# Two-block transformer kernel: rotated query and key rows turned by DMA through HBM and VectorE's 32x32 block transpose

## The reference

```python
h = rmsnorm(x, g_mix)
z = h @ w_in                                    # 1024 -> 5888
aq, ak, av, rq, rk, rv, rg, ga, gb = jnp.split(z, SPLIT_POINTS, axis=-1)

aq = rope_half(aq.reshape(B, S, 8, 64), pos)    # 8 query heads of 64
ak = rope_half(ak.reshape(B, S, 2, 64), pos)    # 2 key heads of 64
ya = sliding_window_sink_attention(aq, ak, av, sinks) @ w_a

rq = retention_rotation(rq.reshape(B, S, 4, 128), pos)
rk = retention_rotation(rk.reshape(B, S, 4, 128), pos) * (128 ** -0.5)
r = chunkwise_retention(rq, rk, rv)             # scores rq.rk per chunk of 128 rows
```

## Time and profile before

| what | us |
|---|---|
| median of 3 runs | 1018.91 (1018.56 to 1019.53) |
| profiled execution, first to last instruction (span) | 1017.5 |
| PE busy | 1010.2 (99% of the span) |
| DVE busy | 715.8 (70%) |
| ACT busy | 506.0 (50%) |
| POOL busy | 170.8 (17%) |
| SP queue's DMA packets, share of 16 engines | 52.8% |

### The profile page before, as it was taken

One profiled execution on the slowest core, in us unless ns is written; L12 is line 12 of the kernel. 1 busy time (PEld: TensorE's weight loads), 2 busy tenths in 40 slices (PEclk: granted clock), 3 DMA queues, 4 the chain that ended last, 5 costly groups with the idle time before them and its releaser, 6 DMA issues.

```text
span 1017.5 us, 13670 instructions
## 1 busy us (share of the span) xinstructions
PE 1010.2 (99%) x5709; PEld 856.6 (84%) x5709; DVE 715.8 (70%) x819; ACT 506.0 (50%) x624; POOL 170.8 (17%) x129
## 2 busy tenths in 40 slices
PE   9999999999999999999999999999999999999997
PEld 8888788888888888888788888888887899899786
DVE  5767755766566565786755767888877767789974
ACT  6545544355444445454564355444467545554352
POOL 0520010000000000430000011000000139259730
PEclk9999999999999999999999999999999999999999
DMA  9763444555556555554444457556553654345451
GB/s 339 246 218 130 166 166 143 178 175 198 183 198 195 178 169 183 186 207 166 158 134 164 166 145 259 203 196 205 190 188 135 223 192 166 124 164 146 116 187 42
DMA packets 98046, 181.29 MB, mean 178 GB/s; under 512 B 8680, under 2 KB 13888, under 8 KB 97856
## 3 DMA queue, kind: packets, MB, share of 16 engines
q1 hardware_dynamic: 97808, 180.32, 52.8%
q10 hardware_dynamic: 176, 0.09, 0.0%
HBM read 177.02 MB, written 1.05 MB: 175 GB/s over the span
## 4 chain that ended last, share of the span: by engine, by line
PE 96%; DMA 2%; DVE 0%; ACT 0%; SPq 0%; issue 0%; DVEq 0%; ACTq 0%
PE bank L745 14%; PE bank L747 12%; PE bank L748 12%; PE bank L1072 11%; PE bank L770 9%; PE bank L774 8%; PE bank L781 8%; PE bank L1076 6%; PE bank L1154 2%; DMA raw<-in_w_in 2%; PE bank L1378 1%; PE bank L943 1%; PE bank L752 1%; PE bank L762 1%; PE bank L1365 1%; PE bank L772 1%
## 5 line engine op out<-in xcount | busy, mean ns | idle before, releaser
L1863 DVE TENSOR_TENSOR w_lo<-arena,w_hi 128x2048 fp32r<-128x2048 f32 (+1 forms) x80 | 185.3, 2325 | 107.5 <-ACT w_hi L1466 107.1
L1863 DVE TENSOR_TENSOR w_lo<-raw,w_hi 128x2048 fp32r<-128x2048 f32 (+1 forms) x78 | 181.2, 2333 | 92.1 <-ACT w_hi L1466 92.0
L1466 ACT ACTIVATE w_hi<-raw 128x2048 fp32r<-128x2048 f32 (+1 forms) x83 | 157.0, 1892 | 105.4 <-PE bank L748 71.5
L1466 ACT ACTIVATE w_hi<-arena 128x2048 fp32r<-128x2048 f32 (+1 forms) x80 | 151.3, 1891 | 105.1 <-PE bank L748 81.3
L1072 PE MATMUL bank<-hT,w_hi 128*128 128x512 f32 x504 | 123.4, 391 | 0.0
L745 PE MATMUL bank<-w_hi,hT 128*128 128x512 f32 (+1 forms) x296 | 114.1, 386 | 0.0
L1072 PEld LDWEIGHTS bank<-hT,w_hi 128*128 128x128 f32 x504 | 92.2, 188 | 17.5
L2465 POOL TENSOR_TENSOR rstd<-mean,const 128x1 f32<-128x1 f32 (+1 forms) x16 | 9.1, 578 | 557.5 <-DVE mean L1872 388.4
L748 PE MATMUL bank<-w_hi,hT 128*128 128x512 f32 (+1 forms) x256 | 97.9, 382 | 0.0
L747 PE MATMUL bank<-w_lo,hT 128*128 128x512 f32 (+1 forms) x256 | 97.9, 382 | 0.0
L770 PE MATMUL bank<-w_hi,hT 128*128 128x512 f32 (+1 forms) x216 | 84.0, 391 | 0.5 <-ACT arena L1478 0.5
(11 more groups left out here) (350 smaller groups left out, 1899.0 us busy)
## 6 DMA issues: line engine op xcount, KB each, us to landing
arena<-in_w_in SPq DMA_DIRECT2D x22, 1024.0 KB, 5.0
raw<-in_w_in SPq DMA_DIRECT2D x20, 1024.0 KB, 5.0
arena<-in_w_up SPq DMA_DIRECT2D x16, 1024.0 KB, 5.3
raw<-in_w_up SPq DMA_DIRECT2D x16, 1024.0 KB, 5.2
arena<-in_w_down SPq DMA_DIRECT2D x16, 1024.0 KB, 5.0
raw<-in_w_down SPq DMA_DIRECT2D x16, 1024.0 KB, 5.0
raw<-in_e_w_in SPq DMA_DIRECT2D x6, 1024.0 KB, 5.1
arena<-in_e_w_in SPq DMA_DIRECT2D x6, 1024.0 KB, 5.1
```

Source lines behind the costliest of these rows:

```text
L1466: act.activation(w_hi[:, p % SPLIT_RING, :, 0:n], raw_at(p)[:, :, 0:n], copy).then_inc(hi_ready, 1)
L1863: dve.tensor_tensor(w_lo[:, s, :, 0:n], raw_at(p)[:, :, 0:n], w_hi[:, s, :, 0:n].bitcast(F32), ALU.subtract).then_inc(lo_ready, 1)
```

## The change

The rotated rows are no longer turned by PE. The rotations write their results in blocks of 32 columns (block number outermost). The SP queue stores them to two internal tensors in HBM (`r_bounce`, 1 MB for both tiles in one DMA; `a_bounce`, 384 KB for each tile). It then fetches them again with every block of 32 columns in its own strip of 32 partitions (`fetch_blocks`: four DMAs of 32 partitions each for the retention rows, and four for each tile of the attention rows). DVE then turns every 32x32 block in place with one instruction for all retention rows (128 x 2048 elements to `rT`) and one for all attention rows (128 x 1536 to `aT`). `rqT`, `rkT`, `aqT` and `akT` are the same places as before. The 16 and 12 transposes of PE and the seven copies of ACT and DVE from PSUM are gone. PE's window 5 waits for `rT_ready` ahead of the retention scores and for `aT_ready` ahead of the attention scores.

The bounce DMAs are put between weight loads of the SP queue (`blocks_moved`), and the two DVE transposes between weight splits. Everything is done once in each of the two layers, and a layer moves 1.75 MB out and 1.75 MB back.

```diff
--- before.py
+++ after.py
@@ -30,6 +30,9 @@
 RET_HEADS = 4
 RET_QK = 128
 RET_V = 256
+BLOCK = 32
+BLOCKS = P // BLOCK
+A_SLOTS = PAIRS + KV_HEADS
 
 ATT2_HEADS = 4
 ROT2 = 32
@@ -278,7 +281,13 @@
         rkT = area(14336, RET_HEADS, SEQ)
         s_far = area(15360, RET_HEADS * P)
         s_ret = area(15872, T, RET_HEADS * P)
-        ak_twice = area(16896, T, KV_HEADS * 2 * HEAD)
+        rT = area(13312, 2 * RET_HEADS, SEQ)
+        aT = area(11776, PAIRS + KV_HEADS, SEQ)
+        r_moved = area(5632, T * BLOCKS, 2 * RET_HEADS * BLOCK)
+        a_moved = area(15360, T * BLOCKS, A_SLOTS * BLOCK)
+        a_rows = area(16896, T, BLOCKS * A_SLOTS * BLOCK)
+        r_bounce = nc.dram_tensor("r_bounce", [T * P, 2 * RET_HEADS * RET_QK], F32, kind="Internal").ap()
+        a_bounce = nc.dram_tensor("a_bounce", [T * P, BLOCKS * A_SLOTS * BLOCK], F32, kind="Internal").ap()
         probs = area(18432, 2, 384)
         probsT = area(19200, 2, 384)
         rg_tanh = z_ga[:, :, 0:512]
@@ -390,13 +399,12 @@
         turned_lo = sem("turned_lo")
         rot_done = [sem(f"rot_done{t}") for t in range(T)]
         rope_done = [sem(f"rope_done{t}") for t in range(T)]
...
@@ -572,8 +580,10 @@
             o.mark(eng.tensor_tensor(bp[:, :, :, 1], zp[:, :, :, 0], sin, ALU.mult))
             between(1)
             o.settle()
-            o.mark(eng.tensor_tensor(zp[:, :, :, 0], ap[:, :, :, 0], bp[:, :, :, 0], ALU.subtract))
-            eng.tensor_tensor(zp[:, :, :, 1], ap[:, :, :, 1], bp[:, :, :, 1], ALU.add).then_inc(rot_done[t], 1)
+            to = z.rearrange("p (b n d e) -> p n b d e", b=BLOCKS, n=heads, e=2)
+            a5, b5 = (v.rearrange("p n (b d) e -> p n b d e", b=BLOCKS) for v in (ap, bp))
+            o.mark(eng.tensor_tensor(to[:, :, :, :, 0], a5[:, :, :, :, 0], b5[:, :, :, :, 0], ALU.subtract))
+            eng.tensor_tensor(to[:, :, :, :, 1], a5[:, :, :, :, 1], b5[:, :, :, :, 1], ALU.add).then_inc(rot_done[t], 1)
             eng.wait_ge(rot_done[t], l + 1)
 
         def rotate_halves(eng, o, l, t, tmp):
@@ -593,11 +603,12 @@
             o.mark(eng.tensor_tensor(b4[:, :, 0, :], z[:, :, 1, :], sin, ALU.mult))
             o.mark(eng.tensor_tensor(b4[:, :, 1, :], z[:, :, 0, :], sin, ALU.mult))
             o.settle()
-            twice = ak_twice[:, t, :].rearrange("p (v c e d) -> p v c e d", v=KV_HEADS, c=2, e=2)
+            to = a_rows[:, t, :].rearrange("p (c e s d) -> p s c e d", c=2, e=2, s=A_SLOTS)
+            aq, bq = (v[:, 0:Q_HEADS, :, :].rearrange("p (i c) e d -> p i c e d", c=2) for v in (a4, b4))
             for e, op in ((0, ALU.subtract), (1, ALU.add)):
-                o.mark(eng.tensor_tensor(z[:, 0:Q_HEADS, e, :], a4[:, 0:Q_HEADS, e, :], b4[:, 0:Q_HEADS, e, :], op))
+                o.mark(eng.tensor_tensor(to[:, 0:PAIRS, :, e, :], aq[:, :, :, e, :], bq[:, :, :, e, :], op))
                 for c in range(2):
-                    last = eng.tensor_tensor(twice[:, :, c, e, :], a4[:, Q_HEADS:, e, :], b4[:, Q_HEADS:, e, :], op)
+                    last = eng.tensor_tensor(to[:, PAIRS:, c, e, :], a4[:, Q_HEADS:, e, :], b4[:, Q_HEADS:, e, :], op)
                     if e == 0 or c == 0:
                         o.mark(last)
             last.then_inc(rope_done[t], 1)
@@ -655,10 +666,40 @@
                     sp.dma_start(raw_at(p)[:, :, 0:piece.shape[2]], piece).then_inc(raw_landed[RAW_SLOTS[p]], 16)
                 n[0] += 1
 
+            def store_rows(dst, src, done):
+
+                sp.dma_start(dst, src).then_inc(done, 16)
+
+            def fetch_blocks(dst, src, done):
+
+                for b in range(BLOCKS):
+                    at = slice(b * BLOCK, (b + 1) * BLOCK)
+                    sp.dma_start(dst[at, :, :], src.rearrange("(u q) (b x) -> b q u x", q=BLOCK, b=BLOCKS)[b]).then_inc(done, 16)
+
+            def blocks_moved(l, piece):
+
+                if piece == 12:
+                    for t in range(T):
+                        sp.wait_ge(rot_done[t], l + 1)
+                    store_rows(r_bounce.rearrange("(t p) n -> p t n", p=P), z_ret, r_stored)
+                if piece == 13:
+                    sp.wait_ge(r_stored, 16 * (l + 1))
+                    fetch_blocks(r_moved, r_bounce, r_blocks)
+                if piece == 14:
+                    sp.wait_ge(rope_done[0], l + 1)
+                    store_rows(a_bounce[0:P, :], a_rows[:, 0, :], a_stored[0])
+                if piece == 15:
+                    sp.wait_ge(rope_done[1], l + 1)
+                    store_rows(a_bounce[P:2 * P, :], a_rows[:, 1, :], a_stored[1])
+                    for t in range(T):
+                        sp.wait_ge(a_stored[t], 16 * (l + 1))
+                        fetch_blocks(a_moved[:, t * BLOCKS:(t + 1) * BLOCKS, :], a_bounce[t * P:(t + 1) * P, :], a_blocks)
+
             for l in range(DEPTH):
                 for g in range(W_IN_GROUPS):
                     for half in range(2):
                         load(w_in_piece(l, g, half))
+                        blocks_moved(l, 2 * g + half)
                 for c in range(2):
                     load(square_piece(ins["w_a"][l], c, 0))
                 for w in ("w_b", "w_out"):
@@ -964,39 +1005,17 @@
 
                 if l == 0 and g == 1:
                     turn_vectors()
-                if g == 3:
+                if g == 5:
+                    pe.wait_ge(rT_ready, l + 1)
                     if l == 0:
                         pe.wait_ge(vec_ready, 3)
-                    for t in (1, 0):
-                        pe.wait_ge(rot_done[t], l + 1)
-                        for i in range(4):
-                            for j in (2 * i, 2 * i + 1):
-                                c = (j % 2) * SEQ + t * P
-                                last = pe.transpose(TURN[i][:, c:c + P], z_ret[:, t, j * P:(j + 1) * P], ident)
-                            if t == 0:
-                                last.then_inc(ret_turned, 1)
-                if g == 4:
-                    for t in range(T):
-                        pe.wait_ge(rope_done[t], l + 1)
-                    pe.wait_ge(rqT_ready, 2 * l + 1)
-                    for b, src, n in ((2, z_att, 0), (5, z_att, 2), (3, ak_twice, 0)):
-                        for j in range(2):
-                            for t in range(T):
-                                c = j * SEQ + t * P
-                                last = pe.transpose(bank[:, b, c:c + P], src[:, t, (n + j) * P:(n + j + 1) * P], ident)
-                        last.then_inc(att_turned, 1)
-                if g == 5:
-                    pe.wait_ge(rqT_ready, 2 * l + 2)
-                    pe.wait_ge(rkT_ready, 2 * l + 2)
-                    pe.wait_ge(akT_ready, l + 1)
                     for n in range(T):
                         at = slice(n * P, (n + 1) * P)
                         for hd in range(RET_HEADS):
                             last = pe.matmul(bank[:, 3 + n, hd * P:(hd + 1) * P], rkT[:, hd, at], rqT[:, hd, at],
                                              start=True, stop=True)
                         last.then_inc(s_ret_done, 1)
-                    pe.wait_ge(aqT_first, l + 1)
-                    pe.wait_ge(aqT_second, l + 1)
+                    pe.wait_ge(aT_ready, l + 1)
                 if g == 6:
                     pe.wait_ge(s_ret_ready, 2 * l + 1)
                     for hd in range(RET_HEADS):
@@ -1541,16 +1560,6 @@
             def window(l, g):
                 if l == 0 and g == 1:
                     vectors_turned()
-                if g == 3:
-                    for i in range(2):
-                        act.wait_ge(ret_turned, 4 * l + i + 1)
-                        act.activation(rqT[:, 2 * i:2 * i + 2, :].rearrange("p h t -> p (h t)"), TURN[i], copy)\
-                           .then_inc(rqT_ready, 1)
-                if g == 4:
-                    act.wait_ge(att_turned, 3 * l + 1)
-                    act.activation(aqT[:, 0:2, :].rearrange("p i t -> p (i t)"), bank[:, 2, :], copy).then_inc(aqT_first, 1)
-                    act.wait_ge(att_turned, 3 * l + 3)
-                    act.activation(akT[:, :, :].rearrange("p i t -> p (i t)"), bank[:, 3, :], copy).then_inc(akT_ready, 1)
                 if 6 <= g < 6 + PAIRS:
                     n = l * PAIRS + g - 6
                     act.wait_ge(probs_turned, n + 1)
@@ -1968,6 +1977,10 @@
                                                     in1=z_rg[:, t, at], op0=ALU.mult, op1=ALU.mult)
                 last.then_inc(r_ready, 1)
 
+            def turn_blocks(dst, src, slots):
+
+                return dve.transpose(dst.rearrange("p s (u q) -> p u s q", q=BLOCK), src.rearrange("p u (s f) -> p u s f", s=slots))
+
             def window(l, g):
                 if g == 1:
                     dve.wait_ge(const_landed, 16)
@@ -1975,15 +1988,9 @@
                     dve.wait_ge(vec_ready, 3)
                     rotate_pairs(dve, order, l, 0, z_ga, between=lambda part: step(l * PIECES + 2 * AQ + 1 + part))
```

(27 more changed lines are left out.)

## The result

The changed kernel takes **1030.02 us** (median of 4 runs, 1028.68 to 1031.63), the kernel before beside it 1018.82 us (4 runs): a ratio of 1.011, interval 1.0096 to 1.0125. It is slower by 11 us. The profiled execution took 1030.54 us; its span is 1028.6 us, 11.1 us more than before.

The account below looks back on a forecast made before the run. PE, busy 1010.2 of 1017.5 us, was taken as the bound. Transposes -5.8, waits for attention rows +7.6 and +8.1, and later DVE work +1.4 gave +11.3 us: 1030.2 us, range 1019 to 1038.

Parts of the forecast that it names:

- The transposes, -5.8: PE's 28 transposes per layer lie uncovered on its path; removing them saves 5.8 us over both layers.
- No wait ahead of the retention scores: Layer 0: `rT` stands at 67.2, ahead of PE's need at 70.35, so PE doesn't wait.
- The waits, 7.6 + 8.1 = 15.7: PE waits for `aT` ahead of the attention scores, 7.6 us in layer 0 and 8.1 in layer 1.
- 3.2 us per MB in a full queue: Rate for SP queue loads, also taken for the new stores: 3.2 us per MB, 1.2 us per 384 KB.
- the last leg: Layer 0, from tile 1's store landing at 73.7 to its last attention fetch landing at 78.1.
- 5.8 us per MB: Rate of the 32-partition fetches, taken from the convolution's copies; 2.2 us per 384 KB.
- C: Rival: fetches run at full rate, waits are 4.4 and 4.9 us, total 1023.8 us; chance 0.17.
- What is late next: DVE starts decay and softmax 1.45 us later; PE's group RG1 waits 0.7 us for its bank, +1.4 both layers.
- DVE is 1.2 us earlier there: Layer 0: without its two L1980 copies DVE could start its attention rotation at 51.1 instead of 52.23.
- rival B: Each wait of PE also lowers its clock, costing some 2.5 us, 5.0 us in all: 1035.2 us; chance 0.27.
- D: Rival: stores avoid the loads' path and fetches run fast, so all is hidden: 1013.1 us; chance 0.10.
- E: Rival: block transpose takes twice the assumed pass, `aT` 1.7 us later per layer: 1033.6 us; chance 0.06.

Follow-up runs that it names:

- e3: The changed kernel without stores and fetches, DVE turning the rotated rows where they stand, so scores come from wrong rows: 1012.4 us.
- e2: The kernel before, with only the retention rows turned the new way and the attention rows still turned by PE: 1015.29 us.
- e5: The kernel before, with only attention rows turned the new way, stores behind load 13, fetches behind load 14: 1016.16 us.
- e7: The changed kernel in its own order, each fetch over 128 partitions instead of 32, giving wrong rows: 1026.96 us.
- e1: The changed kernel with 22 (layer 0) and 29 (layer 1) spare matmuls ahead of PE's wait for aT: 1026.09 us.
- e9: The changed kernel with 128-partition fetches (wrong rows) and all stores and fetches ahead of load 14: 1014.75 us.
- e4: The changed kernel with both attention stores ahead of load 14 and the attention fetches ahead of load 15: 1023.79 us.
- e6: The changed kernel with all stores and 32-partition fetches ahead of load 14: 1020.02 us.

## Why the prediction was right

The mechanism of the waits was right: PE waits for the attention rows, which come late through a full queue, and for nothing else. The clock that the waits cost, 5.9 us, was left out. The total was nearly exact (1030.2 against 1030.02), and that is luck: three of its terms were off, and the errors nearly cancelled.

- **The transposes, -5.8.** Right. e3 shows -6.3 for all that goes, e2 -3.4 for the retention half (3.3 by the earlier trace rows) and e5, by its ratio, -2.9 for the attention half (2.5).
- **No wait ahead of the retention scores.** Right: `rT` at 66.1, wanted at 69.1.
- **The waits, 7.6 + 8.1 = 15.7.** They are 5.4 + 7.1 = 12.5. The step that was mis-sized is "3.2 us per MB in a full queue": it came from two loads 2.2 us apart, the first of which found the queue empty. In the full queue of layer 0 it is 2.6. Counted from load 12's issue, load 14 lands 0.9 us earlier than forecast, load 15 1.7, tile 1's store 1.8, the last fetch 2.5 us. The last 0.7 us are in the last leg, which the forecast took as 0.75 MB at 5.8 us per MB, 4.4 us. Tile 0's fetches were issued 3.6 us before tile 1's store landed, not behind it, and tile 1's own took 3.7 us, which is what the forecast's bound with fast fetches had there (four issues and a landing of 2.1 us). In layer 1 load 15 was late, and the errors are smaller. The 5.8 us per MB of the 32-partition fetches were right within 5% where they are a rate: 5.5 and 5.7 for the retention fetches, and e7's 3.0 shows that the width is its cause. C, full-rate fetches, is refuted by this.
- **"What is late next", +1.4.** Nothing of it shows in the changed kernel. The step took PE at full pace behind the wait, and PE is at half pace there. In e1, where it is at full pace, 0.7 us of waits appear ahead of RG1, for weights from ACT and not for the bank of L2117, so neither the size nor the place was right.
- **"DVE is 1.2 us earlier there."** It is not. Its attention rotation does begin behind the split of piece 9, but its first instruction takes 2.19 us, where it took 1.00 us:

```profile
50.02 2.19 DVE L600 TENSOR_TENSOR arena<-arena,const 128x640 f32<-128x640 f32 x1
```

It now begins 1.9 us after POOL's instruction of the same line (48.15, 3.38 us long) and runs beside it. In every run in which DVE's two copies ahead of it are gone it takes 2.19 or 2.20 us, in e5, where they stand, 1.00. Load 14 was issued 1.2 us later than forecast for it, which cost nothing, as the queue was full until 63.8.
- **The clock.** This is the term that the forecast put at 0; rival B priced it at 2.5 us per wait. From the first retention score of layer 0 to the first matmul of window 6 (L1015 to L1022) the kernel after takes 22.24 us, before (L995 to L1003) 13.79: 8.45 us more, of which 5.40 are the wait and 3.05 are clock. Layer 1 gives 9.98 = 7.09 + 2.89. Together 5.9 us. So B was not a rival but a part of what happened, and e1, by keeping the clock, gets 3.9 us back. The error of choosing 0 was hidden by the 3.2 us that the waits were too long, by the 1.4 us, and 1.5 us of small gains. The sum in terms that were measured is -5.8 + 12.5 + 5.9 - 1.5 = 11.1, the last term being the earlier end of the slow start (0.5), the missing wait at 31.6 (0.5) and a rest of 0.5 that no run explains. The Trainium skill, "TensorE: Matmul & The Clock Gate", part 1, has this mechanism, a throttle that returns after idleness, and the trace agrees: the clock fell in each layer with a wait of 3.6 us or more. The evidence for it in the earlier trace rows was seen and given 0.27; it deserved more.
- **D and E.** The stores take the queue's time: load 13 lands at 58.2, 11.6 us after load 12's issue, where 11.5 were forecast with the store counted and 8.5 without; in e3, which has no store, it is 8.5. The block transposes take 2.31 and 1.78 us, as a plain pass of DVE does, not twice that. The Trainium skill's price of a single block ("VectorE: DVE Perf Modes", section on the three transpose paths), from which an estimate of 3.7 us came, is for bf16. It doesn't carry over to one wide instruction on 4-byte elements: the trace has 1.78 us, and it decides.

What stays open: why the clock stays down for 3.4 us in one case and 6.8 or 10.2 in others; what made load 15 late in layer 1; whether another DMA queue than the SP queue would have carried the trip sooner, which no run tried; how much of e9's 2.3 us over e3 beyond the 1.6 us of waits is anything but the scatter of starts.

## What to carry to other kernels

Moving PE work to a chain of stores and fetches pays only for the part whose last landing is ahead of PE's need; find that by walking the queue in its order, with each load's gate, and move one half where both don't fit (e2 wins 3.4 us, the whole loses 11). Price a wait of PE as the wait plus lost clock: here waits of 3.6 to 7.1 us cost 1.7 to 3.0 us on top, not in proportion to their length. Or give PE spare matmuls for the time. Before reshaping a DMA look at its outermost dimension as well as its number of partitions, and don't count on time won in one transfer when the next issue waits for something else.

## What the runs showed of the hardware that was not expected

- The clock falls with short waits of PE: 3.7 and 3.6 us in e4 (down for 3.4 and 6.8 us), 5.0 and 5.5 us in e7 (6.8 both times), 5.4 and 7.1 us in the change (6.8 and 10.2). What it cost on top of the wait is 1.7 and 2.9, 2.3 and 1.7, 3.0 and 2.9 us, measured as above from the first retention score to window 6. In e6 it also fell in layer 1, 0.2 us behind the end of a wait of 1.8 us ahead of group RG1 (the wait of 0.8 us was 16 us earlier), but not behind the 2.1 us of layer 0; in e9 a wait of 1.1 us left it up. Spare matmuls inside the wait keep it up (e1). The stretch of e6 (PE busy, then clock):

```profile
470.00:475.00 5.00, 3.24 (x25) 0.99 0.02 4
475.00:480.00 5.00, 5.00 (x17) 0.67 0.93 280
```

- A fetch of 256 KB to 32 partitions takes 1.4 us in a full queue, to 128 partitions 0.74 us. With an outermost dimension of four 91 and 65 GB/s are left of the 403 GB/s that the loads reach (the stretch from 82 to 84 us in the changed kernel).
- A block transpose of 4-byte elements over 128 x 2048 takes DVE 2.31 us, about what a subtraction of that size does (2.25 to 2.29), so all 128 partitions are turned in blocks of 32 for the price of one pass.
